# Hybrid streaming encoder step: indexer on 96 rows, an own slot for the last stream's values, rotary copies on GpSimd, and another order of the latent attention's preparation

## What is computed

```python
# A: forgetting attention ("fox"), 6 heads of 64, cached keys and values for the running streams
s = einsum('bqhd,bshd->bhqs', q, FK) * FOX_DIM ** -0.5 + cum_q - cum_k
ya = einsum('bhqs,bshd->bqhd', softmax(where(kpos <= qpos, s, -inf)), FV)
# B: indexer-sparse attention ("dsa"): 8 index heads of 32 choose the keys
sc = einsum('bqhe,bse->bqhs', iq_b, IK) * IDX_DIM ** -0.5
score = einsum('bqhs,bqh->bqs', relu(sc), iw_b)          # then top-k
# C: multi-head latent attention ("mla"): 6 heads, nope 64 + rotary 32
qc = rms(cqa) @ mla_wqb ;  kv = ckv @ mla_wkvb           # expand
q = [rms(qc_nope), rope(rms(qc_pe))] ; k = [rms(kv_nope), kpe] ; v = kv_v
x += (ga * ya + gb * yb + gc * yc) @ w_o ;  x += swiglu(rms(x))
```

## Time and profile before

| | us |
|---|---|
| three runs | 2185.26, 2175.99, 2184.93; median 2184.93 |
| profiled execution | 2179.45 |
| its span in the trace | 2177.6 |
| PE busy | 2122.0 (97%) |
| DVE busy | 1381.3 (63%) |
| ACT busy | 969.5 (45%) |
| POOL busy | 390.0 (18%) |

### The profile page before, as it was taken

The page is one execution under the profiler, slowest core; times in us unless marked ns, Lnnn a source line. Parts: engine busy times, 40 slices in busy tenths (PEclk is TensorE's granted clock), DMA queues, the critical chain, the costliest instruction groups (busy, mean ns, idle before and its releaser), DMA issues.

```text
span 2177.6 us, 36802 instructions
## 1 busy us (share of the span) xinstructions
PE 2122.0 (97%) x13632; PEld 1883.8 (87%) x13632; DVE 1381.3 (63%) x2753; ACT 969.5 (45%) x2068; POOL 390.0 (18%) x283
## 2 busy tenths in 40 slices
PE   9999999999999999999999999899999999999999
PEld 8997767887989989989899877687889799899897
DVE  4566775645838938838445667666467488397493
ACT  4246666556425414314232466665563353243241
POOL 1120020200004314314011200203000042142230
PEclk9999999999999999999999999999999999999999
DMA  6233224233322222222232332241423222222222
GB/s 214 82 105 121 71 69 132 70 98 128 107 98 77 88 78 78 88 78 88 77 135 75 108 113 87 75 135 53 142 75 134 78 78 88 78 88 87 68 97 78
DMA packets 90681, 207.83 MB, mean 95 GB/s; under 512 B 20676, under 2 KB 46920, under 8 KB 90184
## 3 DMA queue, kind: packets, MB, share of 16 engines
q1 hardware_dynamic: 90504, 205.48, 28.5%
HBM read 181.50 MB, written 23.95 MB: 94 GB/s over the span
## 4 chain that ended last, share of the span: by engine, by line
PE 89%; DVE 4%; ACT 3%; issue 2%; DVEq 1%; POOL 1%; DMA 0%; SPq 0%; ACTq 0%
PE ps L849 28%; PE ps L889 15%; PE ps L1339 8%; PE ps L1341 8%; PE ps L1340 8%; PE ps L898 7%; PE ps L1054 2%; PE ps L1071 2%; PE ps L972 1%; PE ps L998 1%; PE ps L953 1%; POOL rsq L1862 1%; PE ps L1160 1%; DVEq L1910 1%; PE ps L1115 1%
## 5 line engine op out<-in xcount | busy, mean ns | idle before, releaser
L1400 ACT ACTIVATE w_hi<-raw 128x1024 fp32r<-128x1024 f32 (+4 forms) x172 | 171.1, 997 | 420.2 <-PE ps L849 369.5
L1917 DVE TENSOR_TENSOR w_lo<-raw,w_hi 128x1024 fp32r<-128x1024 f32 (+4 forms) x124 | 139.1, 1123 | 195.5 <-ACT w_hi L1400 191.9
L889 PE MATMUL ps<-h_hi,w_hi 128*128 128x320 f32 x768 | 246.5, 321 | 1.4 <-ACT g L1400 1.4
L889 PE MATMUL ps<-h_hi,w_lo 128*128 128x320 f32 x768 | 237.4, 309 | 0.0
L889 PE MATMUL ps<-h_lo,w_hi 128*128 128x320 f32 x768 | 237.3, 309 | 0.0
L1339 PE MATMUL ps<-th_hi,op_hi 128*128 128x320 f32 x640 | 198.6, 310 | 3.9 <-issue 3.9
L1862 POOL TENSOR_TENSOR rsq<-ssq,mhalf 128x12 f32<-128x12 f32 (+3 forms) x56 | 118.8, 2122 | 456.1 <-DVE ssq L1995 392.6
L1341 PE MATMUL ps<-th_hi,op_lo 128*128 128x320 f32 x640 | 198.7, 310 | 0.0
L1340 PE MATMUL ps<-th_lo,op_hi 128*128 128x320 f32 x640 | 198.5, 310 | 0.0
L849 PE MATMUL ps<-w_hi,act_hi 128*128 128x512 f32 x440 | 174.5, 396 | 0.0
L849 PE MATMUL ps<-w_hi,act_lo 128*128 128x512 f32 x440 | 174.4, 396 | 0.0
(11 more groups left out here) (367 smaller groups left out, 5319.7 us busy)
## 6 DMA issues: line engine op xcount, KB each, us to landing
raw<-in_weights SPq DMA_DIRECT2D x212, 512.0 KB, 3.3
gates<-gst SPq DMA_DIRECT2D x72, 160.0 KB, 1.8
g<-gates SPq DMA_DIRECT2D x12, 960.0 KB, 7.0
raw<-in_weights SPq DMA_DIRECT2D x24, 384.0 KB, 3.0
ktb<-in_cache_fox_kt SPq DMA_DIRECT2D x16, 384.0 KB, 4.0
vc<-in_cache_fox_v SPq DMA_DIRECT2D x16, 384.0 KB, 3.7
x_sb<-in_x_prompt SPq DMA_DIRECT2D x8, 512.0 KB, 4.8
out_y_prompt<-x_sb SPq DMA_DIRECT2D x8, 512.0 KB, 3.4
```

What stands on the lines that cost most here:

```text
L889: mm = pe.matmul(ps[:, 5, 0:HALF], w[:, kk * P:(kk + 1) * P], h_pair[x][:, kk, half * HALF:(half + 1) * HALF], start=kk == 0 and n == 0, s ...
L1400: return act.activation(dst, src, ACT.Copy, scale=scale)
L1917: dve.tensor_tensor(low[:, 0:width], raw[raw_slot(c)][:, 0:width], high[:, 0:width].bitcast(F32), ALU.subtract).then_inc(lo_made.sem, 1)
```

## The change

It has five parts.

1. The index scores of a pair are made by two split-product matmuls on 96 rows: the queries' three strips are (high, high, low), the keys' (high, low, high), so one matmul gives the three products. New for it: DVE splits the queries (`index_split`, three small instructions, in the even step), PE transposes them (`index_turn`, two transposes, in the odd step), ACT moves them to `qs`. The pair then stands two steps later than before. Keys stand in `kst`, and ACT's move of the DSA stage writes 96 rows of it; the eight query transposes of that stage fall away. DVE makes the keys' low half there with one more instruction for each prompt tile.
2. `mla_turn` is cut: the queries' transposes stay ahead of the turn and the values of the step, the keys' come behind them, and `mla_latent` behind those.
3. `mla_expand` comes last in its step: on PE after the gate half, on ACT after exp, on DVE after the other parts and w_lo.
4. The values of stream 7 get a slot of their own, vc[2]. SP loads it in step 31, ahead of stream 5's load, after the turn of tile 4.
5. The two rotary copies are made by POOL, as soon as the cached rotary keys have landed.

The core of the diff:

```diff
 for _n in range(len(IX_JOBS)):
-    SIDE[_n - _n % 2].append(("index", _n))
-    SIDE[_n - _n % 2 + 1].append(("index_sum", _n))
+    SIDE[_n - _n % 2 + 2].append(("index", _n))
+    SIDE[_n - _n % 2 + 3].append(("index_sum", _n))
+for _n in range(len(IX_JOBS) // 2):
+    SIDE[2 * _n].append(("index_split", _n))
+    SIDE[2 * _n + 1].append(("index_turn", _n))
...
+                    if step == I_FOXS + 7:
+                        sp.wait_ge(tp_done.sem, tp_done.at(L, JOB["mla_turn", TT - 1] + 4))
+                        own_wait(sp, sp_tick)
+                        sp.dma_start(vc[2][:, :, :], past("fox_v", DECB - 1)).then_inc(vc_in[2].sem, 16)
                     b = step - (I_FOXS + 2)
-                    if 2 <= b < DECB:
+                    if 2 <= b < DECB - 1:
...
-                        pe.matmul(ps[:, bank, 0:(t + 1) * P], xt13[r, h // 4, t * P:(t + 1) * P],
-                                  xt13[r, 2, 0:(t + 1) * P], start=True, stop=True).then_inc(tp_done.sem, 1)
+                        if n % 2 == 0:
+                            moved(JOB["index_turn", n // 2] + 1)
+                        pe.matmul(ps[:, bank, 0:(t + 1) * P], qs[:, n // 2 % 2, n % 2, :], kst[:, 0:(t + 1) * P],
+                                  start=True, stop=True).then_inc(tp_done.sem, 1)
+                    if kind == "index_turn":
+                        pe.wait_ge(iq_split.sem, iq_split.at(L, n + 1))
+                        transposes(j, [iq3[:, s, e, :] for e in range(2)])
...
-                    half = (len(SIDE[step]) + 1) // 2
-                    for kind, n in SIDE[step][:half]:
-                        beside(kind, n)
+                    parts = [part for part in SIDE[step] if part[0] != "mla_expand"]
+                    turned = [n for kind, n in parts if kind == "mla_turn"]
+                    half = len(parts) if turned else (len(SIDE[step]) + 1) // 2
+                    for kind, n in parts[:half]:
+                        if kind != "mla_latent" or not turned:
+                            beside(kind, n)
...
-                    for kind, n in SIDE[step][half:]:
+                    for n in turned:
+                        beside("mla_turn_keys", n)
+                        for kind, m in parts:
+                            if kind == "mla_latent":
+                                beside(kind, m)
+                    for kind, n in parts[half:]:
                         beside(kind, n)
                     for k in GATES_IN[step]:
                         gate_half(k)
+                    for kind, n in SIDE[step]:
+                        if kind == "mla_expand":
+                            beside(kind, n)
...
-                    if kind == "mla_rope":
-                        act.wait_ge(rope_in.sem, rope_in.at(L, 16))
-                        copy(rope_keys[n][:, :, :], rope_raw[:, 4 * n:4 * n + 4, :]).then_inc(rope_high.sem, 1)
...
+                        pool.wait_ge(rope_in.sem, rope_in.at(L, 16))
+                        for k in range(2):
+                            pool.tensor_copy(rope_keys[k][:, :, :], rope_raw[:, 4 * k:4 * k + 4, :]).then_inc(rope_high.sem, 1)
```

More of the change, by code:

```diff
@@ L167 @@
     SIDE[I_MLAS - 13 + _k].append(("mla_rope", _k))
[L168 to L169 removed]
+_ORDER = ("index_sum", "foxs_out", "mlas_out", "dsas_out", "mla_streams", "mla_turn", "mla_rope", "mla_absorb", "mla_norm", "mlas_norm", "mlas_keys", "mla_latent",
+          "foxs", "dsas_keys", "index", "index_turn", "index_split", "pick", "mla_expand")
 for _side in SIDE:
@@ L175 @@
 _JOBS_OF = {"foxs_out": 1, "mlas_out": 1, "dsas_out": 1, "mla_streams": 1, "mla_turn": 4, "mla_absorb": 2, "mla_expand": 4, "mlas_keys": 2, "mla_latent": 1,
-            "index": 1}
+            "index": 1, "index_turn": 1}
 JOB, JOBS = {}, 0
@@ L371, in build_program @@
         gate_new = home("gate_new", [102, P], BF16)
-        vc = [home(f"vc{k}", [P, 2, FH * HD], F32, "vc", 3072 * k) for k in range(2)]
+        vc = [home(f"vc{k}", [P, 2, FH * HD], F32, "vc", 3072 * k) for k in range(2)] + [home("vc2", [P, 2, FH * HD], F32, "bias")]
         kpe = home("kpe", [P, TT, ROPE])
@@ L472, in build_program @@
         lfr_made, grow_made = sig("lfr_made", 1), sig("grow_made", 1)
-        vc_in = [sig(f"vc_in{k}", 16 * DECB // 2) for k in range(2)]
+        vc_in = [sig(f"vc_in{k}", 16 * (DECB // 2 - k)) for k in range(2)] + [sig("vc_in2", 16)]
         ktb_in, ctb_in = ([sig(f"{n}{k}", 16 * DECB // 4) for k in range(4)] for n in ("ktb_in", "ctb_in"))
@@ L1183, in _ @@
                     transposes(j, [p_d[:, t, n * P:(n + 1) * P] for n in range(2)])
-                    transposes(j + 1, [block(bkrep[:, t, :, :], 0), p_i[:, t, 0:P], p_i[:, t, P:2 * P], block(ikrep[:, t, :, :], 0)])
+                    queries = [p_i[:, t, 0:P], p_i[:, t, P:2 * P]] if t == TT - 1 else []
+                    transposes(j + 1, [block(bkrep[:, t, :, :], 0)] + queries + [block(ikrep[:, t, :, :], 0)])
                     if t == 0:
@@ L1228, in index_scores @@
                         r = slice(IDM * j, IDM * j + IDM)
-                        mm = pe.matmul(ps[:, j, PAST:PAST + P], zi[r, i, :], xt13[r, 2, SEQ:NTOK], start=False, stop=True)
+                        mm = pe.matmul(ps[:, j, PAST:PAST + P], zi[r, i, :], xt13[r, 2, :], start=False, stop=True)
                     mm.then_inc(ix_done.sem, 4)
@@ L1566, in beside @@
                         move(j, lambda b: act.activation(relu[:, s, 0:w], b[:, 0:w], ACT.Relu))
+                    if kind == "index_turn":
+                        move(j, lambda b: copy(qs[:, s, :, :], b[0:3 * IDM, 0:2 * P].rearrange("p (k c) -> p k c", k=2)))
                     if kind == "mla_latent":
@@ L1628, in xt_parts @@
                         copy(xt0[:, rows], b[:, 0:P])
-                        return copy(xt13[:, :, rows], b[:, P:4 * P].rearrange("p (k c) -> p k c", k=3))
+                        if t < PT_TILES:
+                            return copy(kst[:, rows], b[0:3 * IDM, P:2 * P])
+                        return copy(xt13[:, :, :], b[:, P:4 * P].rearrange("p (k c) -> p k c", k=3))
                     move(JOB["dsa", t] + 1, xt_parts)
@@ L2035, in dsa_norm @@
                     dve.tensor_copy(bkrep[:, t, :, :], rows_bcast(k, 2))
-                    step(dve.tensor_copy(ikrep[:, t, :, :], rows_bcast(ik, 4))).then_inc(dsa_ready.sem, 1)
+                    if t == TT - 1:
+                        step(dve.tensor_copy(ikrep[:, t, :, :], rows_bcast(ik, 4))).then_inc(dsa_ready.sem, 1)
+                    else:
+                        step(dve.tensor_copy(ikrep[:, t, :, :].bitcast(F32R), rows_bcast(ik, 4)))
+                        step(dve.tensor_tensor(ikrep[:, t, 1, :].bitcast(F32R), ik, ikrep[:, t, 1, :], ALU.subtract)).then_inc(dsa_ready.sem, 1)
                 def fox_sums(t):
@@ L2191, in beside @@
                             step(dve.tensor_tensor(edge, edge, cst("fchunk"), ALU.add))
+                    if kind == "index_split":
+                        t, h = IX_JOBS[2 * n]
+                        q, parts = p_i[:, t, IDM * h:IDM * h + 2 * IDM].rearrange("p (h d) -> p h d", h=2), iq3[:, s].rearrange("p h (c d) -> p h c d", c=3)
+                        if n >= 2:
+                            dve.wait_ge(tp_done.sem, tp_done.at(L, JOB["index_turn", n - 2] + 1))
+                        dve.tensor_copy(parts[:, :, 0, :].bitcast(F32R), q)
+                        step(dve.tensor_copy(parts[:, :, 1, :].bitcast(F32R), q))
+                        dve.tensor_tensor(parts[:, :, 2, :].bitcast(F32R), q, parts[:, :, 0, :], ALU.subtract).then_inc(iq_split.sem, 1)
                     if kind == "pick":
@@ L2295, in _ @@
                             lo(C_GATE + 2 + k // 2, k // 2 % 2)
+                    for kind, n in SIDE[it]:
+                        if kind == "mla_expand":
+                            beside(kind, n)
                 at_split(3, 3, at_mla)
```

49 lines of the change are left out of this document (31 added, 18 removed).

## The result

| | us |
|---|---|
| before, 20 runs | median 2182.09 (2175.99 to 2185.26) |
| after, 20 runs | median 2187.84 (2185.95 to 2190.05) |
| ratio | 1.003, 95% interval 1.0023 to 1.0037 |
| profiled execution of after, its span | 2187.3 |

The forecast was 2187 us, +3 on the profiled execution, with the stream steps losing 5.3 a layer and the rest gaining 3.8. The medians say +5.75. Two executions of over 4000 us that stand beside the experiments, one of before and one of the kernel of experiment 4, are left out of all numbers.

The account below looks back on a forecast made before the run. PE, busy 97%, bounds the kernel, except the stream steps, bound by a chain over ACT, DVE, GpSimd and a DMA. Terms -1.6 - 0.9 - 1.26 + 5.3 = +1.5 a layer, +3 in all: 2187 us, 8-in-10 range 2168 to 2199.

Parts of the forecast that it names:

- stream steps: Stage of stream items: later start, longer loop over DVE and GpSimd, later loads; +5.3 us a layer, between +4.9 and +6.0.
- Indexer: Index score pairs on PE: cheaper matmuls less added transposes and waits for ACT; net -1.6 us a layer, bounds -4.2 to +0.5.
- DSA stage: Eight query transposes fewer on PE and a shorter ACT move: -0.9 us a layer, between -1.1 and -0.4.
- Rotary copies: Moving them from ACT to GpSimd frees a turned tile PE waits for: -1.26 us a layer, bounds zero and 1.26.
- slow matmuls: Matmuls below full rate behind the longer wait for stream 5's values: may add up to 1.3 us.
- Its start: In the stream steps, the first expansion moves later on PE, so the first sums come 2.0 to 2.3 us late.
- The loop: In the stream steps, sums from tile to tile go from 8.18 to 9.99 us apart on DVE: +2.4 a layer.
- The queue: On SP, stream 7's load ahead of stream 5's: +0.45 us for the issue, up to +1.3 if both share the engines.
- Rival A: Stream stage not bound by DVE and GpSimd, so PE's holes close: -8.8 us a layer, some 2167; chance 0.14.
- Rival C: Index pair costs two of the old, since row groups side by side are given up: 2218 us; chance 0.02.
- rival B: Stream chain lengthens, and copies and slow matmuls cost their upper ends: +7.4 us a layer, 2200; chance 0.12.
- D: Indexer's matmuls vanish from PE, but PE only waits there for ACT: +3.1 us a layer, 2191; chance 0.08.

Follow-up runs that it names:

- experiment 4: The changed kernel with DVE's sums ahead of query copies and pick, and stream 7's load issued behind stream 6's: 2178.18 us, ratio 0.9985.
- experiment 1: The changed kernel with cut turn, late expansion and own slot undone, index scores and rotary copies kept as changed: 2171.06 us, ratio 0.996.
- 2: The changed kernel with DVE's sums of squares put back ahead of the query copies and the pick: 2180.94 us, ratio 0.9995.
- 3: The changed kernel with stream 7's load issued behind stream 6's instead of ahead of stream 5's: 2179.92 us, ratio 0.9993.
- experiment 5: The kernel of experiment 1 with the cut turn put back and the expansion behind the keys, ahead of the gate half: 2172.7 us, ratio 0.9961.

## Why the prediction was right, and where a term was off

- **The number is nearer than its working.** Two misses cancel in 2187 against 2187.84: the three runs that it starts from have their median 2.8 above that of twenty, and the change was put at +3 (on 2184.93 that makes 2187.9, where 2187 was written) and is +5.75. That part is luck.
- **The direction and the mechanism held.** PE's own savings counted outside the stream steps and were lost inside them; experiment 1 shows the split, and 2 and 3 the two causes named for the loss.
- **Indexer: -1.6 forecast, -2.0 to -3.0 measured in the fox steps.** The last pair, 1.26 before, has left these steps for step 24; by experiment 1, whose stream steps take 69.5 us against a mean of 69.6 before, it costs nothing there that can be seen. A pair takes 0.54 where 0.57 was said. The waits for the queries' copy, forecast as 1.3 (two of 0.5, three of 0.1), are 1.23 in one layer (0.26, 0.49, 0.49) and 2.4 in the other, where w_hi waits for its weights. That case was not in the sum. It was in no bound either as a mechanism, only as a size. (The bounds of this term come out as -4.1 and +0.3 by the prediction's own terms, not -4.2 and +0.5.)
- **DSA stage: -0.9 forecast, -0.7 measured.** Part of the saving became a wait for the move of DSA's own queries (qtd), 0.33 and 0.24.
- **Rotary copies: -1.26 forecast, -1.45 measured.** GpSimd makes both in 2.90 us here (2.24 in the second layer), but only from 363.87 on, when the cached keys land, when ACT made the first one, too; the split on DVE still finds them done.

```profile
363.87 2.90 POOL L1900 CAST rope_keys<-rope_raw 96x1024 fp32r<-96x1024 f32 x2 [44.86 <-DMA rope_raw<-in_cache_mla_kpet]
```

- **Stream steps: +5.3 forecast (4.9 to 6.0, and up to 1.3 for slow matmuls), +7.5 measured.** This is the term that was too small. Along the chain of the first traces (+8.0 and +8.7 in the two layers) it comes apart as follows. Its start was right: the first sums stand 8.1 us behind the scores of step 24, +1.7 and +2.1 where 2.0 to 2.3 was said. The loop was put at +2.4 and is +3.5 and +3.2: three of its steps are the 9.9 to 10.1 of the working, the fourth is 11.0 (10.8 in the second layer), because the gate half of step 26, which was to fit just under it, didn't: PE waited 1.92 for tile 0's norm and then ran slowly for a while (1.49 for six transposes), and the expansion came 0.79 late. The queue was put at 0.45 to 1.3 and is 1.7 and 2.0 (0.49 for the issue, 1.25 and 1.47 for the landing): the two parts were taken as alternatives, and they add. What is left, 1.0 and 1.5, lies behind stream 5's values, in slow matmuls. The wait for these values itself, which was to be about 4 us, is 2.97 and 3.18.
- **The slow matmuls** were put behind the wait for stream 5 alone. They stand behind three waits of after, those of 1.92, 3.02 and 2.97. They make up most of the 3.2 us a layer by which PE is busy for longer, where up to 1.3 was said; not all of that is on the chain. And before pays for them too, in some executions, which a single trace could not tell.
- **Rival A** is out by the sums' distances and by experiment 5: closing PE's holes gave nothing by itself. Rival C is out by the pair's 0.54. Of rival B the stage's part came (+7.5 against its +7.3), but not its losses elsewhere. D is out: the fox steps are shorter.

## What to carry to other kernels

Ask of each stage which engine's order closes the loop before giving a busy engine fewer holes: here PE's holes lay in a loop over DVE and GpSimd, and moving two small DVE parts from under the root into that loop cost more than all holes were worth. A buffer of its own helped the load that was late, issued ahead of what delayed it; given to another load it made the late one later. After a repair, look for the next late thing in the same place: the cut turn, the queries' copy and the first moved load each handed all or part of their gain on to the wait behind.

## What the runs showed of the hardware beyond that

- PE's granted clock behind a wait: in the 5 us behind waits of 1.97, 2.01, 2.09, 2.51 and 2.97 us it was 0.66, 0.50, 1.00, 0.50 and 0.50 on average, and behind waits of 1.92 and 1.93 before the same transposes 0.67 and 1.00. The length of the wait alone doesn't tell it. Such a wait cost up to 2.6 us more than it lasted.
- Of two loads of cached values of 384 KB, issued 0.5 us apart behind a weight chunk, the second landed after 5.1 to 5.8 us in the two traces of after; issued next behind the chunk, the same load landed after 3.8 to 4.3 us in the two of before.
- GpSimd's copy of 96 x 1024 with conversion took as long as ACT's, 1.04 us, for the second of each pair; the first took 1.04 to 1.91 (1.91 and 1.04 in the 2.90 above).
